# The opening of a two-block fp32 kernel reordered, and the border to its convolution FFN in halves

## What is computed

```
mod_l = silu(c) @ w_mod + b_mod              # 6 x 1024: sh1, sc1, g1, sh2, sc2, g2
mod_c = silu(c_ctx) @ w_mod + b_mod
pl = (rmsnorm(x,   norm1_w) * (1 + sc1)  + sh1)  @ w_in
pc = (rmsnorm(ctx, norm1_w) * (1 + sc1c) + sh1c) @ w_in
q, k = silu(dwconv2d(pl[q, k columns]))      # 3x3, image of 8 x 64; v, o and 16 gate columns stay as they are
ml = mlstm(q, k, v, gates from pc, then pl)  # both directions; cumulative sums and maxima of the gates
out = head_rmsnorm(ml) * sigmoid(o)
hg = ...                                     # a second recurrence on further columns of w_in
x = x + g1 * (concat(out, hg) @ w_out)
x = x + g2 * conv_ffn(rmsnorm(x, norm2_w) * (1 + sc2) + sh2)
```

## Time and profile before

| | |
|---|---|
| median of 3 runs | 3072.35 us (3071.69 to 3072.89) |
| profiled execution: its time / its span | 3072.54 us / 3070.7 us |
| mean granted TensorE clock | 0.999 |
| PE matmul / weight load busy | 3031.3 / 2503.2 us |
| DVE / ACT / POOL busy | 1334.7 / 582.0 / 2034.2 us |
| DMA | 300.33 MB, mean 98 GB/s |

### The profile page before, as it was taken

The page is one execution under the profiler, slowest core; times in us unless marked ns, Lnnn a source line. Parts: engine busy times, 40 slices in busy tenths (PEclk is TensorE's granted clock), DMA queues, the critical chain, the costliest instruction groups (busy, mean ns, idle before and its releaser), DMA issues.

```text
span 3070.7 us, 38639 instructions
## 1 busy us (share of the span) xinstructions
PE 3031.3 (99%) x14563; PEld 2503.2 (82%) x14563; DVE 1334.7 (43%) x1574; ACT 582.0 (19%) x927; POOL 2034.2 (66%) x1499
## 2 busy tenths in 40 slices
PE   7999999999999999999999999999999999999999
PEld 5878877888888888877888888888888878888887
DVE  5763366887263322363353331333223652443321
ACT  4451252211121101231011100101001320111000
POOL 3515565888777767554777777777776546777764
PEclk9999999999999999999999999999999999999999
DMA  5202252222333323422223223333234223233222
GB/s 220 83 28 64 97 204 82 97 96 84 95 107 98 96 85 105 123 96 69 96 95 97 95 84 94 110 96 96 84 94 141 90 69 96 96 96 96 91 85 84
DMA packets 323078, 300.33 MB, mean 98 GB/s; under 512 B 6652, under 2 KB 316924, under 8 KB 319264
## 3 DMA queue, kind: packets, MB, share of 16 engines
q1 hardware_dynamic: 319056, 290.55, 29.9%
q10 hardware_dynamic: 3920, 8.36, 0.9%
HBM read 292.60 MB, written 2.10 MB: 96 GB/s over the span
## 4 chain that ended last, share of the span: by engine, by line
PE 94%; DVE 2%; POOL 1%; DMA 1%; issue 1%; ACT 1%; SPq 0%; DVEq 0%; POOLq 0%; ACTq 0%
PE pm L2251 25%; PE pm L2253 25%; PE pm L2252 25%; PE pa L2251 2%; PE pa L2253 2%; PE pa L2252 2%; PE pm L2281 1%; PE pm L2320 1%; PE pm L2321 1%; PE pm L2322 1%; PE pm L2588 1%; DMA modraw<-in_w_mod 1%; PE pm L2285 1%; PE pa L2535 1%; POOL hkeys L803 1%
## 5 line engine op out<-in xcount | busy, mean ns | idle before, releaser
L713 POOL TENSOR_TENSOR wlo<-raw,whi 128x512 fp32r<-128x512 f32 (+1 forms) x1088 | 1434.1, 1349 | 22.7
L709 POOL TENSOR_SCALAR whi<-raw 128x2048 fp32r<-128x2048 f32 (+1 forms) x272 | 478.7, 1760 | 944.8 <-PE pm L2253 597.9
L2251 PE MATMUL pm<-hh,whi 128*128 128x512 f32 x2280 | 895.0, 393 | 5.2 <-DVE mt L2214 2.8
L2253 PE MATMUL pm<-hh,wlo 128*128 128x512 f32 x2280 | 887.8, 389 | 0.0
L2252 PE MATMUL pm<-hl,whi 128*128 128x512 f32 x2280 | 887.7, 389 | 0.0
L2251 PEld LDWEIGHTS pm<-hh,whi 128*128 128x128 f32 x2280 | 428.2, 188 | 98.3 <-issue 5.7
L2252 PEld LDWEIGHTS pm<-hl,whi 128*128 128x128 f32 x2280 | 428.2, 188 | 90.9 <-issue 3.1
L2253 PEld LDWEIGHTS pm<-hh,wlo 128*128 128x128 f32 x2280 | 428.1, 188 | 89.1
L2251 PE MATMUL pm<-uh,whi 128*128 128x512 f32 x880 | 343.1, 390 | 0.7 <-POOL wlo L713 0.7
L2253 PE MATMUL pm<-uh,wlo 128*128 128x512 f32 x880 | 342.5, 389 | 0.0
L2252 PE MATMUL pm<-ul,whi 128*128 128x512 f32 x880 | 342.5, 389 | 0.0
(11 more groups left out here) (481 smaller groups left out, 3887.6 us busy)
## 6 DMA issues: line engine op xcount, KB each, us to landing
...
```

Of the source, the lines that this page charges most:

```text
L709: nc.gpsimd.tensor_scalar(h, r, 1.0, 1.0, ALU.mult, ALU.mult).then_inc(hi_done, 1)
L713: last = nc.gpsimd.tensor_tensor(o[:, c], r[:, c], h[:, c].bitcast(F32), ALU.subtract)
L2251: nc.tensor.matmul(out, wh, ah, start=start, stop=False)
L2253: return nc.tensor.matmul(out, wl, ah, start=False, stop=stop)
```

## The change

- SP loads the scale half of each `w_mod` tile first (512 KiB each), then the first two slabs, then, when the first halves have landed, the shift halves, and the context last.
- Slab 0 is now `mo` (first half). It is multiplied from `x*scale*rstd` without the shift. The shift's product with `w_in` is made apart, by 16 products of one column (`opening_shift`), and added by ScalarE when it takes the result out of the accumulator; the sigmoid follows later, from SBUF.
- The shift's parts of the modulation lie between the chunks of slab 0. Behind it `hh` and `hl` are made anew with the shift for slab 1 (`mq`, `slab_second`) and all others.
- The context's squares go in two large instructions and one reduction, its sum inside slab 2, its `ch` and `cl` beside slab 2.
- The slabs are now 0 `mo`, 1 `mq`, 2 `mv`, 3 and 4 gates, 5 `mq`, 6 and 7 `mk`, 8 `mv`, 9 `mo`, and the banks follow.
- At the border the last chunk of x, its square, the sum, Ln and Exp go in halves of 256 tokens, eleven products on `ident` follow the sum, and the first slab of the FFN takes `hh*whi`, `hh*wlo` of a chunk first and `hl*whi` last.

```diff
-IN1 = ([("mq", 0), ("mv", 2 * ML_W), ("gate", 0), ("gate", 1), ("mq", SLAB), ("mo", 3 * ML_W), ("mk", ML_W),
+IN1 = ([("mo", 3 * ML_W), ("mq", 0), ("mv", 2 * ML_W), ("gate", 0), ("gate", 1), ("mq", SLAB), ("mk", ML_W),
         ("mk", ML_W + SLAB), ("mv", 2 * ML_W + SLAB), ("mo", 3 * ML_W + SLAB)]
        + [(n, HG_AT + o + e) for n, o in (("hq", 0), ("zf", ML_W), ("zb", 2 * ML_W), ("hv", 3 * ML_W), ("hg", 4 * ML_W)) for e in (0, SLAB)])
-MV_AT, GATE_AT, MO_AT, CONV_SLABS = (1, 8), 2, (5, 9), (0, 4, 6, 7)
+MV_AT, GATE_AT, MO_AT, CONV_SLABS = (2, 8), 3, (0, 9), (1, 5, 6, 7)
...
-    p_ = (0, 1, 0, 0, 1, 0, 1, 0, 1, 0)[i_] if i_ < 10 else i_ % 2
+    p_ = (0, 1, 0, 0, 0, 1, 0, 1, 0, 1)[i_] if i_ < 10 else i_ % 2
...
-    sp.dma_start(cx[:].rearrange("p k t -> p (k t)"), io["ctxT"]).then_inc(ctx_loaded, 16)
 
     wm = io["w_mod"][0].rearrange("(k p) n -> k p n", p=P)
     for k in range(KD):
-        sp.dma_start(modraw[k][:], wm[k][:, 0:MOD_W]).then_inc(mod_loaded[MOD_GROUP[k]], 16)
+        sp.dma_start(modraw[k][:, 0:D], wm[k][:, D:2 * D]).then_inc(mod_loaded[MOD_GROUP[k]], 16)
     sp.dma_start(raw[0][:].rearrange("p k n -> p (k n)"), io["w_first"]).then_inc(raw_loaded[0], 16)
+    sp.dma_start(raw[1][:], slab_view(io["w_in"], 0, IN1[1][1])).then_inc(raw_loaded[1], 16)
+    for g in range(4):
+        sp.wait_ge(mod_loaded[g], 16 * MOD_GROUP.count(g))
+    for k in range(KD):
+        sp.dma_start(modraw[k][:, D:2 * D], wm[k][:, 0:D]).then_inc(mod_loaded[k // 2], 16)
+    sp.dma_start(cx[:].rearrange("p k t -> p (k t)"), io["ctxT"]).then_inc(ctx_loaded, 16)
...
+    opening_rstd(0, std, T)
+    act.wait_ge(opening, 1)
+    nc.scalar.activation(modrow[0][:, 0:D // 4], pm[1][:, 0, 0:D // 4], ACT.Copy).then_inc(mod_in, 1)
+    for k in range(KD):
+        act.wait_ge(xn_done, k + 1)
+        nc.scalar.activation(hh[:, k, :], pa[2 + k % 2][:], ACT.Copy).then_inc(hh_done, 1)
     act.wait_ge(mod_used, KD)
-    nc.scalar.activation(modrow[0][:], pm[1][:, 0, :], ACT.Copy).then_inc(mod_row, 1)
+    nc.scalar.activation(modrow[0][:, D // 4:D // 2], pm[1][:, 0, D // 4:D // 2], ACT.Copy).then_inc(mod_row, 1)
+    act.wait_ge(ctx_loaded, 16)
+    act.sem_inc(sq_done, KD - 2)
+    for e in range(2):
+        some = slice(KD // 2 * e, KD // 2 * e + KD // 2)
+        nc.scalar.activation(csq[:, some, :], cx[:, some, :], ACT.Square).then_inc(sq_done, 1)
     act.wait_ge(mod_done, 3)
...
+    for k in range(KD):
+        act.wait_ge(hn_done, k + 1)
+        if k < KD - 1:
+            act.wait_ge(opening, OPENING_TURNED + k + 1)
+        else:
+            act.wait_ge(slab_used, 2 + 1)
+        nc.scalar.activation(hh[:, k, :], pa[2 + k % 2][:], ACT.Identity, bias=mod_col(0, k)).then_inc(hh_done, 1)
+        if k == 2:
+            act.wait_ge(opening, OPENING_ADDED)
+            nc.scalar.activation(mo_shift[:], pa[1][:, 0:2], ACT.Copy).then_inc(mod_in, 1)
+            act.wait_ge(mod_in, 4)
+            for e in range(2):
+                nc.scalar.activation(mo[:, e, :], pm[0][:, e, :], ACT.Identity, bias=mo_shift[:, e:e + 1]).then_inc(mod_in, 1)
+            act.wait_ge(mod_in, 6)
+            act.sem_inc(pm_free[0], 1)
+    opening_rstd(1, rstd, CT)
+    for k in range(KD):
+        act.wait_ge(hn_done, KD + k + 1)
+        nc.scalar.activation(ch[:, k, :], pa[2 + k % 2][:, 0:CT], ACT.Identity, bias=mod_col(0, k, 1)).then_inc(hh_done, 1)
...
+        if e:
+            act.wait_ge(slab_used, 2 + i + 1)
+        else:
+            act.wait_ge(opening, VALUES_MULTIPLIED)
...
+    act.wait_ge(x_mixed, OUT1_SLABS + 1)
+    nc.scalar.activation(osq[1][:, 0:T // 2], x[:, KD - 1, 0:T // 2], ACT.Square).then_inc(sq_done, 1)
+    act.wait_ge(pm_free[1], UP1_USE)
+    nc.scalar.activation(osq[1][:, T // 2:T], x[:, KD - 1, T // 2:T], ACT.Square).then_inc(sq_added, 1)
+    act.wait_ge(osum_half, 1)
+    nc.scalar.activation(orstd[:, 0:T // 2], pa[0][:, 0:T // 2], ACT.Ln, bias=eps[:], scale=1.0 / D).then_inc(osum_half, 1)
     act.wait_ge(sq_summed, 3)
-    nc.scalar.activation(orstd[:], pa[0][:], ACT.Ln, bias=eps[:], scale=1.0 / D).then_inc(std_done, 1)
+    nc.scalar.activation(orstd[:, T // 2:T], pa[1][:, 0:T // 2], ACT.Ln, bias=eps[:], scale=1.0 / D).then_inc(std_done, 1)
+    act.wait_ge(osum_half, 2)
+    act.wait_ge(pm_free[0], UP1_USE)
...
+    def scaled_x(k, done):
+        nc.vector.scalar_tensor_tensor(pa[2 + k % 2][:], x[:, k, :], wsc[:, 0, k:k + 1], pa[0][:], ALU.mult, ALU.mult).then_inc(done, 1)
+
+    def scaled_ctx(k):
+        nc.vector.scalar_tensor_tensor(pa[2 + k % 2][:, 0:CT], cx[:, k, :], wsc[:, 1, k:k + 1], pa[1][:, 0:CT], ALU.mult, ALU.mult).then_inc(hn_done, 1)
+
+    scaled_x(0, xn_done)
+    for k in range(KD):
+        if k < KD - 1:
+            if k:
+                v.wait_ge(hl_done, k)
+            scaled_x(k + 1, xn_done)
+        v.wait_ge(hh_done, k + 1)
+        nc.vector.tensor_tensor(hl[:, k, :], pa[2 + k % 2][:], hh[:, k, :].bitcast(F32), ALU.subtract).then_inc(hl_done, 1)
+
+    for k in range(2):
+        v.wait_ge(hl_done, KD - 1 + k)
+        scaled_x(k, hn_done)
+    v.wait_ge(mod_turned, 1)
+    turned, bias = mod_turned_of(0)
+    nc.vector.tensor_tensor(modc[:, 0:KD, :].rearrange("p (g t) j -> p t g j", t=2), turned, bias, ALU.add).then_inc(mod_done, 1)
     v.wait_ge(mod_done, 3)
     v.sem_inc(pm_free[1], 1)
...
+    for k in range(KD):
+        v.wait_ge(hn_done, k + 1)
+        v.wait_ge(hh_done, KD + k + 1)
+        nc.vector.scalar_tensor_tensor(hl[:, k, :], pa[2 + k % 2][:], mod_col(0, k), hh[:, k, :].bitcast(F32), ALU.add, ALU.subtract).then_inc(hl_done, 1)
+        if k < KD - 2:
+            v.wait_ge(hl_done, KD + k + 1)
+            scaled_x(k + 2, hn_done)
...
+            if k == KD - 1:
+                for e, done in ((0, x_mixed), (1, pm_free[p])):
+                    part = slice(T // 2 * e, T // 2 * e + T // 2)
+                    nc.vector.scalar_tensor_tensor(x[:, k, part], pm[p][:, t, part], mod_col(2, k), x[:, k, part], ALU.mult, ALU.add).then_inc(done, 1)
+                continue
...
+        if k == KD - 1:
+            return last
+        last.then_inc(opening, 1)
+        if 2 <= k < 6:
+            next(shift)
+            next(shift)
+        if k == 6:
+            pe.wait_ge(mod_row, 1)
+            opening_turn(1, pm[1][:, 1, 0:2 * KD]).then_inc(mod_turned, 1)
+
+def opening_shift():
+
+    pe.wait_ge(mod_done, 3)
+    for i in range(2):
+        for k in range(KD):
+            last = nc.tensor.matmul(pa[1][:, i:i + 1], raw[0][:, k, P * i:P * i + P], modc[:, k, 0:1], start=k == 0, stop=k == KD - 1)
+    last.then_inc(opening, 1)
...
+    def slab_second(b, use):
+
+        for k in range(KD):
+            pe.wait_ge(hh_done, KD + k + 1)
+            for w in (whi, wlo):
+                for i in range(2):
+                    nc.tensor.matmul(pm[use][:, i, :], w[b][:, k, P * i:P * i + P], hh[:, k, :], start=k == 0 and w is whi, stop=False)
+            pe.wait_ge(hl_done, KD + k + 1)
+            for i in range(2):
+                last = nc.tensor.matmul(pm[use][:, i, :], whi[b][:, k, P * i:P * i + P], hl[:, k, :], start=False, stop=k == KD - 1)
...
-    square_sum(0, std, T)
-    idle(8)
     pe.wait_ge(mod_in, 1)
-    for k, _ in enumerate(modulation(0, KD)):
+    for k in range(KD):
+        pe.wait_ge(mod_loaded[MOD_GROUP[k]], 16 * MOD_GROUP.count(MOD_GROUP[k]))
+        last = opening_part(k, 0)
         if k == 3:
-            square_sum(1, rstd, CT)
-        if k == 6:
             idle(4)
-    pe.wait_ge(mod_row, 1)
-    mod_turn(modrow[0], pm[1][:, 1, :])
-    idle(5)
-    for i in range(4):
+            opening_sum(0, std, T)
+        if k >= 5:
+            idle(3)
+    last.then_inc(opening, 1)
+    pe.wait_ge(mod_in, 3)
+    opening_turn(0, pm[1][:, 1, 2 * KD:4 * KD]).then_inc(opening, 1)
+    idle(9)
+    in1(0)
+    opening_shift()
+    for i in range(1, 5):
...
+    for e in range(2):
+        nc.tensor.matmul(pa[e][:, 0:T // 2], ones[:], ostd[:, T // 2 * e:T // 2 * e + T // 2], start=True, stop=False)
+    pe.wait_ge(sq_done, 8 * 2 + KD)
+    nc.tensor.matmul(pa[0][:, 0:T // 2], ones[:], osq[1][:, 0:T // 2], start=False, stop=True).then_inc(osum_half, 1)
+    pe.wait_ge(sq_added, 8 * 2 + KD)
+    nc.tensor.matmul(pa[1][:, 0:T // 2], ones[:], osq[1][:, T // 2:T], start=False, stop=True).then_inc(sq_summed, 1)
+    for _ in range(11):
+        nc.tensor.matmul(pa[2][:, 0:P], ident[:], ident[:], start=True, stop=True)
...
+                pe.wait_ge(hh_done, 8 * 3 + k + 1)
+                for w in (whi, wlo):
+                    for i in range(2):
+                        nc.tensor.matmul(up_bank(q, b, i), w[b][:, k, P * i:P * i + P], hh[:, k, :], start=k == 0 and w is whi, stop=False)
+                pe.wait_ge(hl_done, 8 * 3 + k + 1)
+                for i in range(2):
+                    last = nc.tensor.matmul(up_bank(q, b, i), whi[b][:, k, P * i:P * i + P], hl[:, k, :], start=False, stop=k == KD - 1)
+                continue
```

216 lines of the change are left out of this document (114 added, 102 removed).

## The result

The changed kernel takes 3081.55 us (median of 9 runs, 3078.21 to 3084.81); the kernel before, run on the same chip, 3072.60 us (9 runs, 3071.69 to 3073.70). The ratio is 1.0029, 95% interval 1.0020 to 1.0038: slower by 9.0 us. The forecast was 3075.9 us with 3068.5 to 3080.5 as its range and "no change that can be told" as its likeliest case; it was wrong on both, and the time lies at rival 2's. The profiled execution took 3083.43 us around a span of 3081.6, so it has 10.9 us more than the 3070.7 of before. It lies 1.9 us above its own median; some 2 us of what its marks show belong to this one execution.

A forecast was written before the change was run, and what follows sets the result against it. TensorE, busy 99% of the span, was taken as the bound. Opening -0.2, waits +6.0, clock +0.7 and border -3.0 gave +3.5 us on the span, so 3075.9 us against the median; range 3068.5 to 3080.5.

The forecast's parts named there:

- rival 2: Slower: cover missed in full, scans take 22.1 us, clock low twice, opening gives nothing; +8.7 us, 3081; chance 0.17.
- the opening's sum: Start to gates' end: 9.8 us gained by the earlier first slab, 9.6 paid in TensorE's row; net gain 0.2 us.
- The missing cover itself: Behind the gates: mo's 10.9 us slab no longer covers VectorE; two TensorE waits of 6.0 us together, bounds 0.8 to 8.2.
- The first slab at 28.7: Opening: with only the scale half loaded ahead, the first slab starts at 28.7 us instead of 38.46, bounds 25.5 to 29.7.
- The shift's parts, 3.7 us, with 0.6 for VectorE's pace and 0.5 for the turn: Around slab 0: eight shift parts cost 3.7 us, VectorE's slower chunk pace 0.6, the second half turn 0.5.
- The one-column products, 3.6 us: Opening: the shift through w_in, 16 one-column products in 32 records at 0.11 us each, costs 3.6 us.
- The floor of 25 ns: One-column products: the skill's floor between small matmuls would make 32 records 0.8 us; the forecast kept the row's 0.11 each.
- The gates' end at 86.5: End of the gate slabs: 75.8 before, plus the moved slab's 10.9, less the opening's 0.2, gives 86.5 us.
- The scans, 19.8 us, and the wait of 3.2 at gate_columns: Behind the gates: two directions of 7.3 us plus 5.2 for GpSimd's split of slab 8; TensorE then waits 3.2 us.
- Slab 8 at 51.5 us behind the gates: Second values slab: starts at 138.0 us, when mk's convolution frees its bank, where it could have started at 132.0.
- The clock behind two holes, 0.7 us: Behind the waits at gate_columns and slab 8: two holes of about 3 us may lower the clock; 0.7 us, bounds 0 and 2.
- The border, -3.0: Border to the FFN: first product 1.7 us earlier, 1.4 more from the clock held up; 3.0 us gained, bounds 1.5 and 3.4.

The follow-up runs named there:

- ctx_late: Changed kernel with the second values slab waiting for the context's bank only ahead of its context products; 3078.25 us, +4.8 over the kernel before.
- scan_first: Changed kernel with the first direction's scans ahead of conv(1) in VectorE's list; 3081.07 us, +7.6 over the kernel before.
- mended: Changed kernel with the shift's product made by rows, slab 8's split behind the scans, and the context's bank waited for later; 3070.28 us, -3.0 over the kernel before.
- quiet: Changed kernel with GpSimd starting the split of slab 8 only after both directions' scans; 3076.75 us, +3.5 over the kernel before.
- filled: Changed kernel with 9 products on ident in the wait ahead of gate_columns and 13 ahead of slab 8; 3081.69 us, +8.2 over the kernel before.
- border_only: Kernel before with only the border's edits (halves, eleven products on ident, hh products first); 3069.89 us, -3.3 over the kernel before.

## Why the prediction was wrong, step by step

The step that failed most is the opening's sum: -0.2 us in the forecast, +5.1 in the profiled execution. Its largest missing term is the low clock that comes with the sixteen one-column products (3.1 us in that trace), to which the forecast gave no effect. The second is the wait of slab 8 for the context's bank, which the forecast left out (1.8 us, by ctx_late). The missing cover itself, the largest term of the forecast, was right: VectorE frees the bank 51.3 us behind the gates, against 51.5.

- **The first slab at 28.7** (25.5 to 29.7): 29.91 in the profiled execution, 27.56 to 30.68 in the others with the same opening. The bound was too narrow: the first weights landed between 14.9 and 17.3 us (16.52 here, 0.3 late), the four filling products still met the low clock (the row of 20.09, 0.21 us a record instead of 0.12: 0.5 late), and the last four parts with the fillers among them took 4.6 us instead of 4.0. The granted clock is no help there: the profile gives 1.00 for 14 to 24 us, and only the durations show the lower level.
- **The shift's parts, 3.7 us, with 0.6 for VectorE's pace and 0.5 for the turn**: from the first product to the one-column products the forecast has 10.9 + 4.8 = 15.7 us; they took 16.42 (29.91 to 46.33), and 16.42 again in scan_first. A pair of parts takes 1.07, and the four pairs with the slower products behind them some 4.9 us, by the rows of scan_first and of the changed kernel alike. Mis-sized by 0.7.
- **The one-column products, 3.6 us**: right, by the row of scan_first below, where they took 3.63 at full clock. What failed is that the forecast gave them no effect on the clock. With the fall among them they took 4.43, and 2.4 us more were lost in slab 1. The floor of 25 ns that the prediction weighed against the row, from the Trainium skill, TensorE: Matmul & The Clock Gate, section "Wait — 56ns, not 53.3ns?", was no guide here: a record took 0.11 us (3.63 us for 32).
- **The gates' end at 86.5**: 91.8 (the copy's mark, 92.03, less its hand-over). This is the step that failed most, by 5.3 us: 1.2 for the start, 0.7 for slab 0, 0.7 and 2.4 for the low clock and 0.3 of smaller things. How much depends on the execution. Six of the kernels have the same opening instruction for instruction, with marks of 92.03, 92.09, 92.10, 92.77, 92.74 and 89.81, and a seventh, scan_first, whose clock stayed up. In ctx_late the low stretch was half as long (0.63 and 0.52 in 50 to 54 us), hence its 89.81. The seventh:

```profile
27.56 0.70 PE L2377 MATMUL pm<-hh,whi 128*128 128x512 f32 x2
...
43.98 3.63 PE L2399 MATMUL pa<-modc,raw 128*128 128x1 f32 x32
...
86.44 0.68 ACT L1040 ACTIVATE gi<-pm,col 4x512 f32<-4x512 f32 x1 [5.09 <-PE pa L2335]
```

- That execution ends its gates within 0.3 us of the forecast, but by cancelling: it starts 1.1 us earlier than forecast and loses 0.7 in slab 0 and some 0.2 behind. So the sum was that of the lucky case, and the median is another. The Trainium skill, TensorE: Matmul & The Clock Gate, section "What's actually happening", says that what sets the clock does not start anew with a kernel, so one kernel meets its low level at other places from run to run; these seven traces are in keeping with that, but their loads land at different times too, and no run tells the two apart. The changed kernel's runs scatter over 6.6 us, with a mean granted clock of 0.999 in the two at 3078 us and of 0.997 in the four above 3083; mended, with neither narrow products nor a wait of weight there, scatters over 1.5.
- **The scans, 19.8 us, and the wait of 3.2 at gate_columns**: 19.6 and 2.2 (TensorE came later). Right, with its reason: quiet shows that the 5.5 us above 14.1 are GpSimd's split. That the scans alone were estimated at 14.6 is 0.5 off.
- **Slab 8 at 51.5 us behind the gates**: 53.2. The forecast asked only for the bank `pm` that the convolution frees. The slab has a second wait, for the context's bank of the same pair, and VectorE's four context steps, 1.66 us together, stand ahead of it. It is in the code of both kernels, in `in1` (two waits in a row) and in `conv`; ctx_late measured it at 1.8 us.
- **The clock behind two holes, 0.7 us** (0 to 2): 1.2 to 1.6, all behind the second hole, by the marks beside ctx_late. Within its bounds; that the first hole's fall is free, which filled shows, the forecast had not seen.
- **The border, -3.0**: -2.9 in the profiled executions, -3.3 by border_only. Right in size and cause: 1.5 us earlier, and 1.4 by the clock.
- **The rivals**: the result took rival 2's time, but not its mechanism: the scans did not take 22.1 us. Its sum was +1 for the opening, 8.2 and 2 behind it, -2.5; the profiled executions have +5.1, 7.7 and 1.0, -2.9. My chance of 0.17 for slower was too small, because the opening's three narrow margins (start, pace, clock) all had their bad end on the same side, and I had bounded them one by one.
